# The opening of a two-layer decoder trunk: the first weights' up halves on ScalarE's queue, the first split ahead of x, the first product in another order

## The reference, cut to what matters

```python
def swiglu(x, w_gate, w_up, w_down):
    return (jax.nn.silu(x @ w_gate) * (x @ w_up)) @ w_down

for i in range(DEPTH):
    x = layer_norm(DN_ALPHA * x + 0.5 * swiglu(x, ffn_w_gate[i, 0], ffn_w_up[i, 0], ffn_w_down[i, 0]), ...)
    m = mixer_attention(...) if i % 2 == 0 else mixer_sgu(...)
    x = layer_norm(DN_ALPHA * x + m, ...)
    x = layer_norm(DN_ALPHA * x + 0.5 * swiglu(x, ffn_w_gate[i, 1], ffn_w_up[i, 1], ffn_w_down[i, 1]), ...)
    x = x + jax.nn.sigmoid(x @ ple_w_gate[i]) * (p[i] @ ple_w_proj[i])
```

## Time and profile before

| | us |
|---|---|
| median of 3 runs | 1023.72 |
| the 3 runs | 1022.42, 1023.72, 1024.78 |
| profiled execution, its own time | 1023.21 |
| its span | 1021.7 |
| TensorE matmul busy | 1012.8 (99% of the span) |
| TensorE weight load busy | 836.2 (82%) |
| VectorE busy | 610.1 (60%) |
| ScalarE busy | 448.5 (44%) |
| GpSimd busy | 41.9 (4%) |

### The profile page before, as it was taken

The page is one execution under the profiler, slowest core; times in us unless marked ns, Lnnn a source line. Parts: engine busy times, 40 slices in busy tenths (PEclk is TensorE's granted clock), DMA queues, the critical chain, the costliest instruction groups (busy, mean ns, idle before and its releaser), DMA issues.

```text
span 1021.7 us, 12789 instructions
## 1 busy us (share of the span) xinstructions
PE 1012.8 (99%) x4816; PEld 836.2 (82%) x4816; DVE 610.1 (60%) x716; ACT 448.5 (44%) x523; POOL 41.9 (4%) x55
## 2 busy tenths in 40 slices
PE   9999999999999999999999999999999999999998
PEld 7888888888888888888888888888887888888887
DVE  5655455776478745454677544545778864545574
ACT  5444344346473643434356343434344553434441
POOL 0400000100000000000010000000210100000010
PEclk9999999999999999999999999999999999999999
DMA  8875656355236766565539656564467676465531
GB/s 289 283 230 177 208 171 210 114 178 172 83 110 220 250 204 205 164 205 164 165 128 321 210 165 206 165 212 156 135 194 238 204 250 206 164 207 171 196 124 42
DMA packets 129683, 191.47 MB, mean 187 GB/s; under 512 B 5448, under 2 KB 95816, under 8 KB 129520
## 3 DMA queue, kind: packets, MB, share of 16 engines
q1 hardware_dynamic: 126432, 180.11, 53.9%
q0 software_dynamic: 2928, 10.61, 3.1%
q10 hardware_dynamic: 288, 0.26, 0.1%
HBM read 189.90 MB, written 1.06 MB: 187 GB/s over the span
## 4 chain that ended last, share of the span: by engine, by line
PE 93%; DVE 4%; DMA 1%; ACT 1%; issue 1%; SPq 0%; DVEq 0%; ACTq 0%
PE gu L388 19%; PE gu L390 19%; PE gu L389 19%; PE acc L388 10%; PE acc L390 10%; PE acc L389 10%; PE tp L466 4%; DVE g_lo L1118 2%; DMA rawB<-in_sgu_w_in 1%; ACT g_hi L830 1%; PE acc L653 1%; DVE t_tok L1514 0%; DVE xT_lo L1118 0%; DMA x_tok<-in_x 0%; DVE stage L1505 0%
## 5 line engine op out<-in xcount | busy, mean ns | idle before, releaser
L388 PE MATMUL gu<-g_hi,xT_hi 128*128 128x512 f32 x928 | 363.5, 392 | 1.2 <-DVE xT_lo L1118 1.1
L390 PE MATMUL gu<-g_hi,xT_lo 128*128 128x512 f32 x928 | 361.0, 389 | 0.0
L389 PE MATMUL gu<-g_lo,xT_hi 128*128 128x512 f32 x928 | 360.4, 388 | 0.0
L388 PEld LDWEIGHTS gu<-g_hi,xT_hi 128*128 128x128 f32 x928 | 174.3, 188 | 37.5 <-issue 2.4
L390 PEld LDWEIGHTS gu<-g_hi,xT_lo 128*128 128x128 f32 x928 | 174.2, 188 | 36.2
L389 PEld LDWEIGHTS gu<-g_lo,xT_hi 128*128 128x128 f32 x928 | 174.3, 188 | 34.8
L896 ACT ACTIVATE stage<-gu 128x256 f32<-128x256 f32 x88 | 33.7, 383 | 361.2 <-PE gu L390 361.1
L1118 DVE TENSOR_TENSOR g_lo<-rawA,g_hi 128x2048 fp32r<-128x2048 f32 (+2 forms) x66 | 141.5, 2145 | 78.4 <-ACT g_hi L830 78.3
L1118 DVE TENSOR_TENSOR g_lo<-rawB,g_hi 128x2048 fp32r<-128x2048 f32 (+1 forms) x64 | 141.0, 2203 | 18.1 <-ACT g_hi L830 18.1
L1244 DVE SCALAR_TENSOR_TENSOR stage<-stage,gu 128x256 f32<-128x256 f32 x88 | 37.0, 420 | 189.6 <-ACT stage L896 189.6
L388 PE MATMUL acc<-d_hi,hT_hi 128*128 128x512 f32 x352 | 144.8, 411 | 0.0
(11 more groups left out here) (181 smaller groups left out, 673.1 us busy)
## 6 DMA issues: line engine op xcount, KB each, us to landing
rawD<-in_ffn_w_down SPq DMA_DIRECT2D x44, 1024.0 KB, 4.9
rawA<-in_ffn_w_gate SPq DMA_DIRECT2D x42, 512.0 KB, 4.0
rawA<-in_ffn_w_up SPq DMA_DIRECT2D x42, 512.0 KB, 4.9
rawB<-in_ffn_w_gate SPq DMA_DIRECT2D x42, 512.0 KB, 4.4
rawB<-in_ffn_w_up SPq DMA_DIRECT2D x42, 512.0 KB, 5.5
rawA<-in_attn_w_in SPq DMA_DIRECT2D x12, 512.0 KB, 4.4
rawB<-in_attn_w_in SPq DMA_DIRECT2D x12, 512.0 KB, 4.9
rawA<-in_ple_w_gate SPq DMA_DIRECT2D x8, 512.0 KB, 4.7
```

Of the source, the lines that this page charges most:

```text
L388: pe.matmul(dst, hi[b], w_hi[b], start=first and b == 0, stop=False)
L389: pe.matmul(dst, hi[b], w_lo[b], start=False, stop=False)
L390: done = pe.matmul(dst, lo[b], w_hi[b], start=False, stop=last and b == len(hi) - 1)
```

## The change

Six edits, all in the opening:
- ScalarE issues the up halves of all five pieces: pieces 0 and 1 where they were, pieces 2, 3 and 4 after its table load and its first small activation. SP issues the gate halves alone, so three transfers fewer stand in its list.
- ScalarE and VectorE split piece 0 ahead of x(0,0).
- The bank of x(h,j) is h, so x(1,0) goes to bank 1 and need not wait for bank 0.
- TensorE's second group of dummies has 2 instead of 4.
- The first six matmuls of half 0 come ahead of the transposes of x(1,0) in part (three of them), with the other three behind, ordered by operand.
- The wait for the last parts of x is on `tp_taken[h]` instead of `tp_taken[j]`, as the banks changed.

The number of matmuls of the product, of transposes, of splits and of bytes is the same.

```diff
@@ -38,7 +38,7 @@
 C_ROWS = HD + LO_ROW + HEADS
 ALPHA = (2.0 * DEPTH) ** 0.25
 EPS = 1e-5
-WARM = (6, 4)
+WARM = (6, 2)
 FIRST = [(0, 1), (1, 2), (2, 4), (4, 6), (6, 8)]
 NEG = -1e30
 SCALE = HD ** -0.5
@@ -327,7 +327,7 @@
 
             def load_first(piece):
                 for sources, ks, raw in first_source(piece):
-                    for b, cols, src in (sources[:1] if piece < 2 else sources):
+                    for b, cols, src in sources[:1]:
                         sp.dma_start(raw[:, ks, cols], src[:, ks]).then_inc(raw_q[piece], 16)
 
             load_x(0, 0)
@@ -411,30 +411,41 @@
                         between()
                 done.then_inc(g_done, 1)
 
-            def first_turn(h, j):
+            def first_turn(h, j, bank, use):
 
                 pe.wait_ge(x_loaded[h][j], 16)
-                transposes(j, h, [x_tok[:, h, 512 * j + P * q:512 * j + P * q + P] for q in range(4)])
-
-            def g_first(operand_wait):
+                transposes(bank, use, [x_tok[:, h, 512 * j + P * q:512 * j + P * q + P] for q in range(4)])
+
+            def g_first():
 
                 def first(h, piece):
                     pe.wait_ge(split_q, piece + 1)
                     return g_piece(0, h, gu[h][:, :], *FIRST[piece])
 
-                first_turn(1, 0)
-                operand_wait(0, 0)
-                first(0, 0)
-                first(0, 1)
-                first_turn(0, 1)
-                operand_wait(0, 1)
+                def one(x, b, w, start=False):
+                    pe.matmul(gu[0][:, :], x[:, b, 0:P], w[:, 0, b, :], start=start, stop=False)
+
+                pe.wait_ge(tp_hi[0], 1)
+                pe.wait_ge(split_q, 1)
+                one(xT_hi, 0, g_hi, start=True)
+                one(xT_hi, 0, g_lo)
+                pe.wait_ge(high_q, 2)
+                one(xT_hi, 1, g_hi)
+                first_turn(1, 0, 1, 0)
+                pe.wait_ge(tp_taken[0], 1)
+                one(xT_lo, 0, g_hi)
+                one(xT_lo, 1, g_hi)
+                pe.wait_ge(split_q, 2)
+                one(xT_hi, 1, g_lo)
+                first_turn(0, 1, 0, 1)
+                pe.wait_ge(tp_taken[1], 1)
                 first(1, 0)
                 first(1, 1)
                 first(0, 2)
-                first_turn(1, 1)
+                first_turn(1, 1, 1, 1)
                 first(1, 2)
                 for h in range(HALVES):
-                    operand_wait(1, h)
+                    pe.wait_ge(tp_taken[h], 2)
                     first(h, 3)
                     first(h, 4).then_inc(g_done, 1)
 
@@ -506,7 +517,7 @@
                     pe.matmul(acc[0][:, 0, 0:P], ident[:, :], ident[:, :], start=True, stop=True)
 
             dummies(WARM[0])
-            first_turn(0, 0)
+            first_turn(0, 0, 0, 0)
             dummies(WARM[1])
 
             half1 = half1_block = None
@@ -544,7 +555,7 @@
                         down(c - 1, cs - 1, 1)
 
                     if k == 0:
-                        g_first(x_wait)
+                        g_first()
                     elif PHASES[k - 1][0] == "ple":
                         up(0, 0, 0, half1, x_wait)
                     else:
@@ -867,18 +878,24 @@
                 act.wait_ge(raw_q[piece], 32)
                 copy(g_hi[:, 0, k_from:k_to, :], raw[:, k_from % 4:k_from % 4 + k_to - k_from, :]).then_inc(high_q, 1)
 
-            for piece in range(2):
+            def load_up(piece):
                 for sources, ks, raw in first_source(piece):
                     for b, cols, src in sources[1:]:
                         act.dma_start(raw[:, ks, cols], src[:, ks]).then_inc(raw_q[piece], 16)
+
+            load_up(0)
+            load_up(1)
             act.wait_ge(table_in, 1)
             act.activation(small[:, 147:148], small[:, 146:147], ACT.Silu)
+            load_up(2)
+            load_up(3)
+            load_up(4)
+            hi_first(0)
             xT_high_block(0, 0, 0, bank=0)
-            hi_first(0)
             hi_first(1)
-            xT_high_block(0, 1, 1, bank=0)
+            xT_high_block(0, 1, 0, bank=1)
             hi_first(2)
-            xT_high_block(1, 0, 0, bank=1)
+            xT_high_block(1, 0, 1, bank=0)
             hi_first(3)
             hi_first(4)
             xT_high_block(1, 1, 1, bank=1)
@@ -1213,12 +1230,12 @@
                     g_hi[:, 0, k_from:k_to, :]).then_inc(split_q, 1)
 
             dve.memset(small[:, 146:147], 0.0).then_inc(table_in, 1)
+            lo_first(0)
             xT_low_block(0, 0, 0, bank=0)
-            lo_first(0)
             lo_first(1)
-            xT_low_block(0, 1, 1, bank=0)
+            xT_low_block(0, 1, 0, bank=1)
             lo_first(2)
-            xT_low_block(1, 0, 0, bank=1)
+            xT_low_block(1, 0, 1, bank=0)
             lo_first(3)
             lo_first(4)
             xT_low_block(1, 1, 1, bank=1)
```

## The result

The changed kernel takes 1024.3 us (median of 22 executions, 1023.38 to 1026.32), the kernel before, in 22 executions beside it, 1022.82 (1022.16 to 1024.78). The ratio is 1.0015, 95% interval 1.0009 to 1.002: the change makes the kernel slower by 0.9 to 2 us, less than the 0.2% set out above. In a later series the changed kernel had 1024.34 us and before 1023.09, ratio 1.0012 (1.0003 to 1.0021).

A forecast was written before the change was run, and what follows sets the result against it. TensorE's matmuls, covering 99% of the span, bound the kernel. Dummies, split, banks and issues 0, x(0,1) +0.5 us on the profiled 1023.21 gave 1023.7; the median 0.5 above it gave 1024.2 us, range 1022.3 to 1025.6.

The forecast's parts named there:

- Dummies, split ahead of x, banks, order: Opening up to x(0,1)'s transposes: TensorE arrives 0.9 us sooner, 8.55 for 9.44, but must wait there; each costed at 0.
- Issues: SP and ScalarE: x(0,1) issued at 3.15 instead of 3.66, ScalarE's three new issues from 3.25 to about 4.6; costed at 0.
- The place of x(0,1): DMA line: 128 to 256 more packets go ahead, so x(0,1) lands about 0.5 us later, 9.9 instead of 9.36.
- rival C: Opening: all 768 ScalarE packets ahead of x(0,1), 1.4 us later, 1025.1; with first product at half clock 1027.4; chance 0.06.
- the one for one: DMA line: SP's and ScalarE's queues send equal packet counts while both have work, as 76 and 80 from 3.5 to 4 us.
- the better filling: DMA line: SP's earlier issues buy at most its idle share, 0.06 us from 5 to 6 us.
- Nothing gives it back: After x(0,1) lands at 9.9: the half us stays, bias product at 21.56, down product at 27.5.
- Rival A: After the first product: x(0,1) lands at 8.85, TensorE then waits for VectorE's gating; 1023.5 to 1023.7; chance 0.33.

The follow-up runs named there:

- Experiment 1: Changed kernel with SP again issuing the up halves of pieces 2 to 4; 1023.02 us against 1023.03 of before, ratio 0.9998.
- experiment 2: Kernel before with only the up halves of pieces 2 to 4 moved to ScalarE's queue; 1025.2 us against 1023.03, ratio 1.0019.
- experiment 4: Changed kernel without three matmuls at the end of the first product; 1023.02 us, ratio to before 1.0002.
- experiment 5: Changed kernel with four dummy matmuls ahead of the transposes of x(0,1); 1025.22 us against 1022.6 of before, ratio 1.0026.
- Experiment 9: Kernel before without nine matmuls of the first product (blocks 4 to 6, token half 1); 1023.22 us against 1023.09, ratio 1.0002.
- experiment 6: Changed kernel with SP issuing the up halves of pieces 3 and 4, ScalarE those of 0 to 2; 1022.87 us against 1022.6 of before, ratio 1.0003.
- experiment 12: Changed kernel with ScalarE issuing only the original pieces 0 to 2's up halves, piece 2 cut in two; 1022.89 us against 1023.09 of before, ratio 0.9999.
- experiment 7: Changed kernel with SP issuing x(0,1) ahead of piece 2's gate half; 1024.46 us against 1022.6 of before, ratio 1.0015.
- experiment 3: Kernel before without three matmuls at the end of the first product; 1022.27 us against 1023.03, ratio 0.9991.
- filled twins: Changed kernel with four dummy matmuls ahead of the transposes of x(0,1), run in two series; 1025.22 and 1025.23 us, ratio to before 1.0026 both times.
- experiment 8: Kernel before once more, unedited, for the spread of its own trace; its profiled execution took 1024.51 us and not 1023.21.
- experiment 11: Changed kernel with four dummy matmuls ahead of the transposes of x(0,1), repeated beside the changed kernel; 1025.23 us, ratio to before 1.0026.

## Why the prediction came out as it did

The number held: 1024.2 against 1024.3 measured, and the change is below 0.2%, as expected. That it held to 0.1 us is luck, two errors that cancel: the median of before fell from the 1023.72 of three runs to 1022.82 in 22, and the change costs about 1.5 us in the medians where I had 0.5. The two profiled executions are 1.05 us apart (1024.26 and 1023.21).

**Dummies, split ahead of x, banks, order: costed at nothing.** Right by time. Experiment 1 has all of them and the time of before. The first product started at 6.52 (6.65 forecast), and TensorE was through with the work ahead of the transposes of x(0,1) at 9.04 (8.55 forecast), since x(1,0) held it for 0.40 us: that quarter, too, shared the line with ScalarE's queue.

**Issues.** This step failed in part. I let ScalarE's three issues begin at 3.25, behind the table load and the activation. They began at 1.80, beside it, and were out 1.4 us sooner than the 4.6 that I had.

**The place of x(0,1).** The direction was right: the two queues share the line, and x(0,1) lands later. This is the term that was mis-sized. I counted 384 to 512 packets of ScalarE's queue ahead of x(0,1), 128 to 256 more than before (0.34 to 0.74 us by the rates used there). All 768 were through before it had landed, which is 512 more and 1.4 us by that rate. Measured was +1.03 us (10.39 for 9.36). So it was rival C's packet count, without its clock, with the forecast's outcome.

What was wrong in the count is mainly the one for one. From 5 to 7 us SP's queue sent 187 packets and ScalarE's 390, which is 203 more. The issue times matter less: up to 5 us ScalarE's queue had sent 347 packets, and 288 is what it had in all before, so 59 of the new ones had gone by then. The sum, 262, is about what lies between my upper count and the 768. This is worked out from one trace; no run issues the three transfers later, so the shares of the two causes were not tested.

Nor is the rest of 0.37 us between 1.4 and 1.03 settled. The line moved 0.62 MB from 3 to 5 us instead of 0.56, and 0.34 from 5 to 6 instead of 0.32, which at 350 GB/s is some 0.2 us; I had valued the better filling at 0.06. The landings of `bias_tab` and `rawD`, 0.39 and 0.38 us sooner, would account for all of it, but they move as much between executions with no change in the loads. The difference of x(0,1) itself is beyond that: its transposes' weight loads start at 9.1 to 9.6 us in the five executions with the loads issued as before, and at 10.3 to 11.0 in the five of the changed queues in which nothing else held them (the changed kernel twice, experiments 2, 4 and 5).

The Trainium skill ("DMA: Bandwidth & Descriptors", queues, rings and completion order) says that each engine goes round between the queues that have work, a packet at a time. In the packets that the profile counts, this trace agrees with it where both queues had packets of 1 KB (190 of ScalarE's against 201 from 4 to 5 us). Elsewhere it does not fit: from 5 to 6 us it was 203 packets of ScalarE's against 97, with 55.1% against 44.2% of the time, and from 8 to 9 us 159 against 178, with 44.1% against 64.6%. SP's queue had packets of 2 KB (x) among its own in these two stretches. Neither equal counts nor equal time fits both, so by what the turns are measured stays open.

**Nothing gives it back.** Right but for 0.1 us: +0.90 at the turn, +0.92 at 162 us.

**Rival A's limit** was real. Experiment 9 shows TensorE standing for 1.94 us in front of the gating. Behind a sooner x(0,1) stand limits that I had not named: `xT_lo` of x(1,0) at 9.6 to 9.7 us (experiments 6 and 12) and the split of piece 2 at 11.1 us (experiment 6; 13.3 in experiment 7).

**Rival C, the clock.** At 0.998 were 4 of 33 executions of the changed kernel, 1 of 11 in experiment 2, 2 of 10 in experiment 4: 7 of 54 where TensorE stands still for some 0.8 to 1.2 us in front of x(0,1). Of the 87 executions of before in the experiments' series it was none, of experiments 1, 3, 6 and 12 none of 43, and of the filled twins none of 16. In experiment 9, where TensorE stands still for 1.94 us at 19 us, it was 8 of 10; in experiment 7, with 1.52 us at 12 us, none of 10. For the changed kernel such an execution is some 1.9 us longer (1026.0 to 1026.3). The counts go with the standing still, but not throughout: experiment 7 has none, and the twins have none although TensorE still stood for 0.86 us in the profiled execution of experiment 5. No trace of such an execution was caught, so where the lower clock sits, and what brings it, is not shown. The filled twins do not show that filling helps, since they are slower for all that.

**What stays open.** The opening accounts for 0.92 us and the medians for 1.48 (1.25 in the second series); 0.92 is the lower end of the first interval and lies well inside the second, and the executions at 0.998 add 0.2 on the average (4 of 33 at 1.9), less in a median. Experiment 2, with x(0,1) as late, is 2.2 us above before and the filled twins 2.1 to 2.6, which the openings of their fast executions do not explain either. A first product at the lower pace, as in the twin's trace, is a candidate that no mean clock would show; it was not tested. Later waits of 0.9 us that come in one execution of a program and not in another (experiment 8) are as large as the rest. Whether the change makes them more frequent was not settled.

## What to carry to other kernels

Moving transfers to a second issuing queue does not only save issue time: it lets them overtake. When the line is full, everything on the second queue takes its share at once, so only what is needed early should go there (experiment 6), and what TensorE's next instruction needs should not wait behind it. Before work is drawn forward, look for the operand that comes next after the one that is sped up: here TensorE arrived 0.4 us sooner at a load, and behind that stood `xT_lo` of another quarter of x, a split and a gating, each with less than 0.4 us of room. And judge a step in the opening by the distance between two rows of one execution, since experiments 6 and 12 differ by 0.15 us at the bias product and by 0.01 in that distance.

## What was not expected of the hardware

- The DMA issues on ScalarE's queue did not wait for the table load and the activation ahead of them: the load ran from 1.74 to 3.02 us, the activation from 3.04, and the issues started at 1.80 and 2.23.
- An execution can run its first product at 1.2 GHz until about 10.4 us (0.43 us from matmul to matmul, experiment 11, with a granted clock of 1.00 in the profile), while another of nearly the same program has 0.23 us from 6.8 us on (the changed kernel: 6.83 to 7.06).
- The landing of one and the same load moves by up to 0.7 us between executions without any edit that bears on the loads: the copy of `bias_tab` started at once when it had landed, and it landed at 15.93, 16.18, 16.40, 16.46 and 16.65 in the five executions with the loads issued as before. One profiled execution can't tell effects below that size; the distances between rows of one execution can.
